# The causal mask of attention: from identity products on TensorE to an addition by VectorE in PSUM

## The reference

```python
def one_block(args):
    q_blk, blk = args
    sc = jnp.einsum('bhqd,bhkd->bhqk', q_blk, kh) * scale
    q_idx = blk * ATTN_BLOCK + jnp.arange(ATTN_BLOCK)
    sc = jnp.where(key_idx[None, :] <= q_idx[:, None], sc, -jnp.inf)
    p = jax.nn.softmax(sc, axis=-1)
    return jnp.einsum('bhqk,bhkd->bhqd', p, vh)
```

## Time and profile before

| | |
|---|---|
| three timed runs | 1107.93, 1107.95 and 1108.74 us, median 1107.95 us |
| the profiled execution | 1108.93 us |
| its span, from first to last instruction | 1107.1 us |
| mean granted clock of TensorE | 0.994 of full speed |
| busy: PE, DVE, ACT, POOL | 1081.3, 647.3, 503.8, 47.1 us |
| attention heads, first score product to the first DVE operation behind them | 281.9 to 313.4 us of the span |

### The profile page before, as it was taken

One profiled execution on the slowest core, in us unless ns is written; L12 is line 12 of the kernel. 1 busy time (PEld: TensorE's weight loads), 2 busy tenths in 40 slices (PEclk: granted clock), 3 DMA queues, 4 the chain that ended last, 5 costly groups with the idle time before them and its releaser, 6 DMA issues.

```text
span 1107.1 us, 18807 instructions
## 1 busy us (share of the span) xinstructions
PE 1081.3 (98%) x8329; PEld 987.0 (89%) x8329; DVE 647.3 (58%) x791; ACT 503.8 (46%) x597; POOL 47.1 (4%) x34
## 2 busy tenths in 40 slices
PE   7999999998889999999999999999999999999998
PEld 7999988987789799999889999888788889999986
DVE  5755544688665775555447555544764557555542
ACT  5644433683633354444335444434654536444430
POOL 1000000112051000000000000000100000000000
PEclk9999999999899999999999999999999999999999
DMA  9855555253002356555546565555445474665531
GB/s 311 265 181 187 189 190 178 87 190 114 1 15 68 126 184 189 188 190 191 190 152 194 188 190 191 190 185 176 153 159 218 155 228 154 192 189 190 191 114 38
DMA packets 127194, 184.91 MB, mean 167 GB/s; under 512 B 4205, under 2 KB 101722, under 8 KB 126986
## 3 DMA queue, kind: packets, MB, share of 16 engines
q1 hardware_dynamic: 126368, 181.88, 50.6%
q0 software_dynamic: 448, 1.71, 0.5%
q10 hardware_dynamic: 298, 0.12, 0.1%
HBM read 182.66 MB, written 1.05 MB: 166 GB/s over the span
## 4 chain that ended last, share of the span: by engine, by line
PE 88%; DVE 7%; ACT 2%; issue 2%; DMA 1%; POOLq 0%; SPq 0%; POOL 0%; DVEq 0%; ACTq 0%
PE B L1274 19%; PE B L1275 19%; PE B L1276 19%; PE B L1315 7%; PE B L1319 7%; PE B L1316 7%; PE B L1688 3%; DVE wlo L840 2%; DVE arena L1007 1%; PE B L1384 1%; PE B L1385 1%; PE B L1386 1%; DMA raw<-in_ffn_w_up 1%; PE B L1348 1%; PE B L1811 1%
## 5 line engine op out<-in xcount | busy, mean ns | idle before, releaser
L840 DVE TENSOR_TENSOR wlo<-raw,whi 128x2048 fp32r<-128x2048 f32 (+1 forms) x169 | 387.7, 2301 | 227.5 <-ACT whi L443 227.3
L443 ACT ACTIVATE whi<-raw 128x2048 fp32r<-128x2048 f32 (+1 forms) x171 | 324.2, 1908 | 385.2 <-PE B L1276 243.0
L1274 PE MATMUL B<-xTh,whi 128*128 128x256 f32 x1408 | 397.4, 282 | 0.3 <-DVE wlo L840 0.2
L1275 PE MATMUL B<-xTl,whi 128*128 128x256 f32 x1408 | 396.4, 282 | 0.0
L1276 PE MATMUL B<-xTh,wlo 128*128 128x256 f32 x1408 | 396.4, 282 | 0.0
L1274 PEld LDWEIGHTS B<-xTh,whi 128*128 128x128 f32 x1408 | 266.1, 189 | 1.2 <-DVE wlo L840 0.7
L1275 PEld LDWEIGHTS B<-xTl,whi 128*128 128x128 f32 x1408 | 266.3, 189 | 0.0
L1276 PEld LDWEIGHTS B<-xTh,wlo 128*128 128x128 f32 x1408 | 266.2, 189 | 0.0
L1315 PE MATMUL B<-whi,hTh 128*128 128x512 f32 x352 | 139.5, 396 | 0.0
L1316 PE MATMUL B<-wlo,hTh 128*128 128x512 f32 x352 | 139.0, 395 | 0.0
L1319 PE MATMUL B<-whi,hTl 128*128 128x512 f32 x352 | 110.6, 395 | 0.0
(11 more groups left out here) (241 smaller groups left out, 999.6 us busy)
## 6 DMA issues: line engine op xcount, KB each, us to landing
raw<-in_ffn_w_up SPq DMA_DIRECT2D x44, 1024.0 KB, 5.4
raw<-in_ffn_w_down SPq DMA_DIRECT2D x44, 1024.0 KB, 4.8
raw<-in_ffn_w_gate SPq DMA_DIRECT2D x43, 1024.0 KB, 5.5
raw<-in_sg_w_in SPq DMA_DIRECT2D x16, 1024.0 KB, 5.4
raw<-in_ab_w_in SPq DMA_DIRECT2D x8, 1024.0 KB, 5.1
raw<-in_sg_w_out SPq DMA_DIRECT2D x8, 1024.0 KB, 5.3
raw<-in_ab_w_out SPq DMA_DIRECT2D x4, 1024.0 KB, 4.8
raw<-in_ab_w_in SPq DMA_DIRECT2D x2, 832.0 KB, 4.4
```

The costliest lines, as they stand in the source:

```text
L443: A(whi[:, j % SLOTS, 0:kt * width], raw[:, j % SLOTS, 0:kt * width], ACT.Copy).then_inc(S("hi_ready"), 1)
L840: TT(wlo[:, j % SLOTS, 0:n], raw[:, j % SLOTS, 0:n], whi[:, j % SLOTS, 0:n].bitcast(f32), ALU.subtract).then_inc(S("lo_ready"), 1)
L1274: mm(out_ap, lh, rh, start=first, stop=False)
L1275: mm(out_ap, lh, rl, start=False, stop=False)
```

## The change

The two identity products per head go; each diagonal block is now complete with its one score product. DVE adds the constant to both diagonal blocks with one operation (the constant is read twice, by broadcast), which reads the scores from PSUM and writes them back there, and is linked to the maximum. ACT reads the sums from PSUM as before.

```diff
 def row_max(h):
...
                 src, m = B[SCORE_BANK[h % 2]][:, 0:384].rearrange("p (b n) -> p b n", n=P), smax[:, h % 2, :]
+                link(TT(src[:, 0:2, :], src[:, 0:2, :], bc(const("future").unsqueeze(1), [P, 2, P]), ALU.add))
                 link(nc.vector.tensor_reduce(m, src, AX.X, ALU.max))
...
 def head_scores(h):
...
                     last = mm(o, qTm[0:QK, h, P * tq:P * tq + P], kTm[0:QK, h, P * tk:P * tk + P],
-                              start=True, stop=i == 2)
-                    if i < 2:
-                        mm(o, ident, future, start=False, stop=True)
+                              start=True, stop=True)
                 last.then_inc(S("score_sums"), 1)
```

More of the change, by code:

```diff
@@ L1575, in _ @@
                 last.then_inc(S("gc_sums"), 1)
-            future = const("future")
             def head_scores(h):
```

## The result

The changed kernel is slower: 1110.79 us median of 8 runs (1106.48 to 1112.35) against 1108.18 us for the kernel before (1107.5 to 1108.74, 8 runs), a ratio of 1.0022 with a 95% interval of 1.0012 to 1.0033. So the change costs about 2.6 us, where 0.15 us were forecast, and the median lies above the range (1106.7 to 1109.8). The profiled execution took 1112.35 us with a span of 1110.5 us, 3.4 us more than the span before. Where these lie is read further down: the heads end 0.84 us late, the level loop of the delta rule behind them takes 2.57 us more, and from its end to the end of the span both traces take 756.9 us.

A forecast was written before the change was run, and what follows sets the result against it. In the attention heads PE, DVE and ACT pass each head on, none full; 4.8 us off PE and 3.6 us onto DVE leave -0.3 us; the middle of 1108.6 and 1107.65 us gave 1108.1 us, range 1106.7 to 1109.8 us.

The forecast's parts named there:

- The additions and the products: Attention heads: eight DVE additions at 0.45 us add 3.6 us; sixteen PE products removed save 4.8 us.
- PE's gap: PE's idle between head 1's scores and head 0's transposes grows from 0.83 to 3.0 us.
- head 2: Third attention head: its maximum begins 0.41 us earlier, its result comes 0.04 us later.
- the order of releases: Attention heads: which engine's work releases each maximum; heads 0 and 7 wait for DVE's own work.
- forecast of -0.3 us: Head-by-head sum of shifts at the end of the attention heads: 0.3 us earlier.
- C: Rival, attention heads: clock rises one stretch later, until about 294.3 us; +1.3 us, 1109.4 us; chance 0.12.
- B: Rival, DVE additions: PSUM write is dear, 0.72 instead of 0.45 us on four heads; +1.1 us, 1109.2 us; chance 0.10.
- A: Rival, attention heads: PE decides and the additions hide; 2.2 us saved, 1105.75 us; chance 0.06.
- the second rise of the earlier trace: PE's clock behind the heads: read as falling at about 318.4 us and rising at 321.6 us, used for the later-rise rival.
- head 1: Second attention head: its maximum begins only 0.09 us later, its result 0.54 us later.
- Behind the stage nothing is edited.: Rest of the kernel behind the heads (313.38 us): keeps the heads' shift of -0.3 us.
- the rise at 291 us: PE's clock in the attention heads: goes from 0.50 to 1.00 at 291 us, expected again after the change.

The follow-up runs named there:

- e12: Changed kernel with two 1 MB weight loads issued behind the level loop and 51 products of no use holding the clock: 1110.96 us, ratio 1.0030.
- e11: Kernel before with the same two weight loads issued late and 45 products of no use holding the clock: 1105.6 us, ratio 0.9985.
- e14: Changed kernel with 51 products of no use in PE's four idle places, loads where they were: 1106.7 us, ratio 0.9993.
- e6: Kernel before with 45 products of no use in PE's four idle places to hold the clock: 1104.82 us, ratio 0.9971.
- e2: Changed kernel with all sixteen identity products kept on PE, written to unread spare columns, besides the DVE additions: 1110.59 us, ratio 1.0026.
- e1: Changed kernel run once more without edit: 1110.85 us, ratio 1.0025.
- e3: Changed kernel without the DVE addition, so products removed only and diagonal blocks unmasked: 1109.74 us, ratio 1.0013.
- e4: Changed kernel with six full-size products of no use in PE's gap behind the scores of head 1: 1110.5 us.
- e7: Changed kernel with 51 products of no use (13, 20, 9, 9) and ten tiny ones in PE's four idle places: 1111.52 us.
- e8: Kernel before run once more without edit: 1107.77 us, ratio 0.9999.
- e5: Changed kernel with sixteen tiny two-column products of no use behind the scores of head 1: 1111.85 us.
- e10: Kernel before with the two 1 MB weight loads under the level loop issued late: 1113.88 us, ratio 1.0054.

## Why the prediction was wrong

**The additions and the products: right in size.** The addition costs 0.43 us and 0.45 to 0.47 us with its link; PE's gap, head 2 and the order of releases came as worked out. With the clock out of play the whole change costs the heads 0.14 us (e12 against e11) and 0.15 us (e14 against e6), and the loop nothing (25.35 and 25.36 us in all four). The forecast of -0.3 us was for a clock that rises in mid-stage; with the late rise of the first trace it becomes C's +1.0 us against 0.84 us measured, so the sum was good to some tenths. B is refuted: the write to PSUM adds 0.01 us. A is refuted by the heads of e2 and by these pairs, in which sixteen products less on PE gained the heads nothing. Two readings in the working were off without bearing on this: the second rise of the earlier trace rows lies near 321.9 us (0.63 as the mean of 321.5 to 322.0), which puts C at 294.6 us, and head 1 begins 0.45 - 0.39 = 0.06 us later, not 0.09.

**The step that failed: "Behind the stage nothing is edited."** I ended the sum at 313 us and put the rest of the kernel at nothing. In the traces it is 2.57 us of the 3.4. The change takes 64 instructions from PE's stream, and everything behind stands elsewhere against the weight loads. In the unedited loop five of the traces with a shorter or shifted stream and the loads where they were (changed, e1, e3, e4, e7) show idle without releaser, 0.4 to 2.0 us; the kernel before has none over 0.15 us in two, nor has e2. (Its first trace has a hitch of the same kind: at 340.99 us, 1.3 us behind an instruction transfer, two starts are 0.26 us apart, most of what its loop of 25.64 us is above 25.36.) Setting equal low stretches side by side prices it: loop 28.21 us in the changed kernel against 26.81 (e8) and 26.82 us (e2), 1.4 us; with the clock up through the loop, e7 against e6, 2.4 us.

**The clock: one draw taken for a rule.** The forecast read the rise at 291 us out of one trace, and C priced a later rise inside the heads alone. Over the traces (e5's delay aside) the rise came between 285 and 294 us, and further low stretches came behind the heads in both kernels. Holding the clock is worth 1104.82 against 1107.47 us, 2.65 us, in the kernel before, and 1106.7 against 1110.8 us, 4.1 us, in the changed one. But these last two were not measured side by side, and by the ratios both kernels gain about 0.3% (1 to 0.9971, and 1.0022 or 1.0025 to 0.9993). That the clock takes more from the changed kernel is thus not shown; both gains also hold what the useless products shift in the program. The page TensorE: Matmul & The Clock Gate, section "Why this matters for your kernels", of the Trainium skill, warns of idle gaps between bursts of matmuls. These runs agree: filling them gave the kernel before 0.29% by the ratio (0.24% between the medians).

**What adds up and what doesn't.** With the clock held in both, the changed kernel is behind by 1.3 us (each median against that of the kernel before beside it: -1.3 us for e14, -2.65 us for e6) to 2.4 us (the ratios, 0.9993 and 0.9971, whose intervals just touch). The traces give 0.15 us of that to the work itself, so 1.2 to 2.3 of the 2.6 us are neither work nor the clock's gaps. PE's stops are the one thing found for it; how many come in each execution isn't measured, since e14's trace is of its fastest run. (With the loads moved, e12 is even 5.4 us above e11, at 0.14 us of work between them; behind the loop their traces take 761.2 and 758.3 us.) The two causes aren't cleanly separable either, since the clock fell behind a stop (e12, e10) and a changed clock moves the stop. That the stops go with bulk loads is shown by moving the loads: all but one lie under a load or up to 2.3 us behind one (the exception is 0.21 us at 357.6 us in e7). That PE waits there for its own instructions is inferred, as the profile names no releaser, but on firm ground: the stop falls inside a run of like products, and it always ends 1.2 to 1.6 us behind a transfer of the instruction queue. What holds that transfer up under a load isn't recorded.

Of e2's 2.8 us its one trace gives 1.6 us to additions on the path and 1.2 us to a low stretch of the clock in the loop; the second trace of the kernel before has that stretch as well, and how often either kernel has it isn't known.

## What to carry to other kernels

A small edit in one stage moves the instruction stream of everything behind it. In this kernel, whose PE program is unrolled and whose weight loads fill the DMA engines, that was worth 1 to 2 us; look for idle of PE without a releaser under a bulk load, and for the transfers of the instruction queue ahead of it, before explaining a difference by the edit. Price a stage that hangs at the lower clock from several traces, not one. Where PE must wait for other engines, full-size products into a spare part of a bank can be worth more than the work saved.

## What the runs showed of the hardware

- PE stops in the middle of a row of like products for 0.2 to 2.6 us while loads of 1 MB run at some 350 GB/s or shortly behind them; moving two loads by 20 us moved the stop with them and made the kernel before 6 us slower (e10).
- A DMA queue of the kind "instruction" makes 65 or 66 transfers of 16 KB in a kernel of some 8300 PE products. All 17 stops ended 1.2 to 1.6 us behind the end of one of them; ahead of the longest, in e12, it came 6.6 us behind the one before it.
- Products of no use in four gaps kept the granted clock at 1.00 from 276 to 330 us and made the kernel before 0.29% faster by the ratio (e6, interval 0.18 to 0.40%).
- A product with 128x128 weights and two columns takes 0.21 us a record at the lower clock (6.83 us for 32 records in e5), as much as one with 128 columns.
- DVE adds in place in PSUM at the price of a PSUM read into SBUF: 0.43 us for 128x256.
